# Where the 640 token columns of the split products are parted: 128 + 512 rather than 320 + 320

## The chip, the cores and the metric

The kernel runs on one core of one Trainium2 chip. The metric is the device time of one execution in microseconds. Inside the core five engines run their own instruction streams: TensorE (its matmuls are "PE" in the profile, its weight loads "PEld"), VectorE ("DVE"), ScalarE ("ACT"), GpSimd ("POOL") and SyncE ("SP"), the last of which issues most of the DMAs.

## What is computed

One step of a two-layer backbone over two groups of tokens that share all weights: 128 context tokens and 512 latent tokens, 640 in all, with a model width of 1024.

```python
for l in range(DEPTH):
    h = rmsnorm(x, g_pre_mix[l]) * (1.0 + sc1) + sh1      # sc, sh: one set per token group
    u = h @ w_in[l]                                       # q, k, v of attention; r, k, v of RWKV
    ...                                                   # windowed attention and RWKV scans
    x = x + gt1 * rmsnorm(concat(o_att, o_rw) @ w_o[l], g_post_mix[l])
    h = rmsnorm(x, g_pre_ffn[l]) * (1.0 + sc2) + sh2
    f = (silu(h @ w1) * (h @ w3)) @ w2                    # l = 0: dense, width 2816
    ...                                                   # l = 1: 8 experts of width 1408, top 2 of 8
    x = x + gt2 * rmsnorm(f, g_post_ffn[l])
```

All inputs, weights and outputs are float32. The context and the latent tokens differ in modulation, attention and scan, but the projections and the feed-forward are the same product for all 640.

## The kernel before

**The work and its order.** The phases follow each other: modulation, projection, attention, RWKV mixing, output projection and feed-forward of layer 0, then the same of layer 1 with the experts at the end. The weights stream from DRAM in blocks of 128 x 1024 float32 (512 KB) through a ring of 8 slots in SBUF. SyncE issues one block's DMA as soon as TensorE has counted the block 8 places earlier as used (`block_used`). The order of everything is written out by hand, each engine's stream on its own, tied by semaphores.

**Split products.** Large products do not run as full float32. ScalarE copies a block to the reduced float32 type (`fp32r` in the profile), the upper part (L1702, `w_proj`, `w_ffn`); VectorE subtracts it from the original and writes the lower part over the ring slot (L2278 in the projections and the experts, L2782 in the dense feed-forward, `ring_lo`). Activations are split alike (`hT_hi` or `hT_ffn_hi`, and `hT_lo`, L2284). `mm_split` (L449) then issues three matmuls into the same accumulator: upper times upper (L451), upper weights times lower activations (L452), lower weights times upper activations (L453). Each matmul comes with its own weight load.

**The 640-column helper.** `mm640_split` (L455) calls `mm_split` twice, for columns 0 to 320 and 320 to 640 of the token axis, with the weights as the stationary operand (128 x 128) and the activations as the moving one. Its accumulator is `pair_r(n)` (L445): 640 columns within the two PSUM banks 2n and 2n+1 (512 float32 columns each), columns 192 to 832 of the 1024, so that each half lies in one bank. Who uses the two:

- `proj_phase` of TensorE (L868): 21 blocks in each layer. For block o the 8 slices kc of 128 input channels are multiplied into pair `o % 4`. ScalarE's `proj_phase` (L1739) evicts a block when it has been used (L1750 and the lines after it for whole 640-column rows, L1763 and L1764 for the context and the latent part), and prepares the upper part of the block two further on; VectorE (L2371) reads the same pair once more for the token shift.
- `dense_phase` of TensorE (L1430): layer 0's feed-forward. In groups of 6, 6, 4 and 6 hidden tiles (`FF_GROUPS`) it computes two blocks per tile (w1 and w3), 44 in all, and after each group the down projection (`ff_down`, `ff_last`), which has 128 tokens as the stationary operand and 512 weight columns as the moving one. The pairs are given by `ff_pair`. ScalarE takes tanh of the w1 accumulator (L2096), VectorE combines it with the w3 one.
- `norm_into` (L848): the first block of each projection and of the dense feed-forward is interleaved with the transposes of the normalised input (L845): as soon as a slice kc of the input is transposed, evicted and split, its six products are issued.

The experts of layer 1 go through `mm_split` directly, with 256 moving columns (up) and 512 (down). Products of full float32 that cover all 640 tokens use another helper, `mm640` (L461), which issues 128 columns (L463) and 512 columns (L464).

Of the kernel before, what the change touches and what calls it, by code (L numbers as in the profile page):

```python
# [18 lines left out]
CTX = 128  # L19
LAT = 512  # L20
T = CTX + LAT
# [158 lines left out]
def build(nc, blocks, x_all, small, cond, sinkrows, router, low2, cache_k, cache_v, state, consts,  # L180
          y_all, new_k, new_v, new_state, h_rows, y_rows, h_plain):
    ctx = ExitStack()
    with ctx:
# [251 lines left out]
        def pair(n):  # L435

            return ps[:, 2 * n:2 * n + 2, :].rearrange("p b c -> p (b c)")
# [6 lines left out]

        def pair_r(n):  # L445

            return pair(n)[:, 192:832]

        def mm_split(nc, dst, w_hi, w_lo, m_hi, m_lo, start, stop):  # L449

            nc.tensor.matmul(dst, w_hi, m_hi, start=start, stop=False)  # L451
            nc.tensor.matmul(dst, w_hi, m_lo, start=False, stop=False)  # L452
            return nc.tensor.matmul(dst, w_lo, m_hi, start=False, stop=stop)  # L453

        def mm640_split(nc, n, w_hi, w_lo, h_hi, h_lo, start, stop):  # L455
            for h in range(2):
                sl = slice(320 * h, 320 * h + 320)
                mm = mm_split(nc, pair_r(n)[:, sl], w_hi, w_lo, h_hi[:, sl], h_lo[:, sl], start, stop)
            return mm

# [312 lines left out]
        def _(pe):  # L773
# [74 lines left out]
            def norm_into(k, first, w_h, hi):  # L848

                for kc in range(KC + 2):  # L850
                    if kc < KC:
                        norm_turn(k, kc)
                    j = kc - 2
                    if j >= 0:
                        if j == 0:
                            w_l = first_split()
                        pe.wait_ge(sem["x_lo"], first + j + 1)
                        at = slice(j * P, (j + 1) * P)
                        mm = mm640_split(nc, 0, w_h[:, at], w_l[:, at], hi[:, j, :], hT_lo[:, j, :], j == 0, j == KC - 1)
                done(mm)  # L860
# [7 lines left out]
            def proj_phase(l):  # L868
                norm_into(2 * l, X_PROJ[l], w_proj[:, used[0] % 2, :], hT_hi)
                for o in range(1, PROJ_B):  # L870
                    w_h, w_l = split_blk(w_proj)
                    n = l * PROJ_B + o
                    if o >= 4:
                        pe.wait_ge(sem["proj_ev_act"], n - 3)
                    if 6 <= o - 4 < 18:
                        pe.wait_ge(sem["proj_ev_dve"], 13 * l + o - 9)
                    for kc in range(KC):
                        k = slice(kc * P, (kc + 1) * P)
                        mm = mm640_split(nc, o % 4, w_h[:, k], w_l[:, k], hT_hi[:, kc, :], hT_lo[:, kc, :], kc == 0, kc == KC - 1)
                    done(mm)  # L880
# [549 lines left out]
            def dense_phase(l):  # L1430
                norm_into(2 * l + 1, X_FFN[l], ffn_high(used[0]), hT_ffn_hi)
                for g, (f0, f1) in enumerate(FF_GROUPS):
                    for f in range(f0, f1):
                        for w in range(2):
                            if f == 0 and w == 0:
                                continue
                            w_h, w_l = ffn_high(used[0]), first_split()
                            if f >= f0 + 2:
                                pe.wait_ge(sem["eh_g"], f - 1)
                            elif g >= 1:  # L1440
                                pe.wait_ge(sem["ff_dn"], 2 * NT * (g - 1) + 4 + 2 * (2 * (f - f0) + w))
                            for kc in range(KC):
                                k = slice(kc * P, (kc + 1) * P)
                                mm = mm640_split(nc, ff_pair(g, f, w), w_h[:, k], w_l[:, k], hT_ffn_hi[:, kc, :], hT_lo[:, kc, :], kc == 0, kc == KC - 1)
                            done(mm)
                    if g < len(FF_GROUPS) - 1:
                        ff_down(g, f0, f1)
                    else:
                        ff_last(g, f0, f1)
# [231 lines left out]
        def _(act):  # L1681
# [57 lines left out]
            def proj_phase(l):  # L1739
# [4 lines left out]
                for o in range(PROJ_B):  # L1744
                    act.wait_ge(sem["block_used"], first + o + 1)
                    if o + 2 < PROJ_B:
                        w_hi(w_proj, first + o + 2)
                    src = pair_r(o % 4)
                    if o < 4:
                        A(qT[:, o, :], src, ACT.Copy, scale=HD ** -0.5).then_inc(*E.sig("proj_ev_act"))  # L1750
                    elif o == 4:
                        A(kT[:, :], src, ACT.Copy).then_inc(*E.sig("proj_ev_act"))
                    elif o == 5:
                        A(vT[:, :], src, ACT.Copy).then_inc(*E.sig("proj_ev_act"))
                    elif o < 18:
                        j = o - 6
                        pr = praw[:, j % 2, :]
                        if j < 2:
                            for z in (0, 129, 642):
                                A(pr[:, z:z + 1], C("ones")[:, 0:1], ACT.Copy, scale=0.0).then_inc(*E.sig("act_step"))  # L1760
                        else:
                            act.wait_ge(sem["proj_ev_dve"], 13 * l + j - 1)
                        A(pr[:, 1:129], src[:, 0:CTX], ACT.Copy, scale=hpar[:, j:j + 1]).then_inc(*E.sig("act_step"))  # L1763
                        A(pr[:, 130:642], src[:, CTX:T], ACT.Copy, scale=hpar[:, j:j + 1]).then_inc(*E.sig("proj_ev_act"))  # L1764
                    elif o == 18:
                        A(zlow[:, 0, :], src, ACT.Tanh).then_inc(*E.sig("proj_ev_act"))
                    elif o == 19:
                        A(zlow[:, 1, :], src, ACT.Copy).then_inc(*E.sig("proj_ev_act"))
                    else:
                        A(zlow[:, 2, :], src, ACT.Tanh, scale=0.5).then_inc(*E.sig("proj_ev_act"))  # L1770
# [316 lines left out]
            def dense_phase(l):  # L2087
                first = FFN_AT[l]
                ff_w_hi(first + 2)
                for g, (f0, f1) in enumerate(FF_GROUPS):  # L2090
                    for f in range(f0, f1):
                        n = ff_blocks(g) + 2 * (f - f0)
                        act.wait_ge(sem["block_used"], n + 2)
                        if f >= 2:
                            act.wait_ge(sem["eh_g"], f - 1)
                        A(ftmp[:, f % 2, :], pair_r(ff_pair(g, f, 0)), ACT.Tanh, scale=0.5).then_inc(*E.sig("eh_th"))  # L2096
                        ff_w_hi(n + 3)
                        act.wait_ge(sem["eh_g"], f + 1)
                        A(g_hi[:, f - f0, :], g_f[:, f - f0, :], ACT.Copy).then_inc(*E.sig("eh_hi"))
                        ff_w_hi(n + 4)  # L2100
                    if g < len(FF_GROUPS) - 1:
                        for d in range(f1 - f0):
                            ff_w_hi(ff_blocks(g) + 2 * (f1 - f0) + d + 3)
# [1161 lines left out]
```

## Time and profile before

| | us |
|---|---|
| median of 2 runs | 2722.01 |
| lowest and highest | 2722.01 and 2722.01 |
| the profiled execution | 2724.16 |
| its span, first to last instruction | 2722.3 |
| mean granted clock of TensorE, share of full | 0.975 |

A record of a matmul or of a weight load begins when the hardware starts it and ends when it is through the array; the ends of matmuls are modelled, and successive records overlap. The distance between two starts is therefore a different quantity from the duration of one record. "f32" in a matmul's row stands for full and reduced float32 alike; which of the two it is follows from the line: L451 to L453 are the reduced type. A full float32 product appears as two records. In the waits, "A <- B" reads: A waited, and B ended it.

### The profile page before, as it was taken

Reading aid. Unit: us, or ns where it says so; the run is one execution under the profiler, and the core shown is the slowest. Engines: PE = TensorE matmul, PEld = TensorE weight load, DVE = VectorE, ACT = ScalarE, POOL = GpSimd, SP = SyncE. Lnnn points to the kernel's source line nnn. Section 1 sums busy time; section 2 is a strip of 40 time slices with the busy share of each in tenths; the row PEclk is TensorE's granted clock in tenths of the full one; section 3 lists DMA queues with packets and bytes.
Section 4 is the critical chain, followed back from the end, with each engine's and each line's share of the span. In section 5 each row is a group of like instructions: output and inputs, shape, how many; then the busy total and the mean of one; then the engine's idle time right before and its main releaser. Section 6 shows DMA issues by size and latency. Waiting matters only on the chain.

```text
span 2722.3 us, 68039 instructions
## 1 busy us (share of the span) xinstructions
PE 2521.7 (93%) x30324; PEld 2197.1 (81%) x30324; DVE 1401.3 (51%) x2474; ACT 1128.5 (41%) x2126; POOL 146.1 (5%) x163
## 2 busy tenths in 40 slices
PE   6998799898899999989987999998999999999996
PEld 3996577676798999969965777766899999999995
DVE  2337455556533333362374665474565555555565
ACT  3226544544421211242255545444444444444452
POOL 0002000010000000010010010001000000000011
PEclk8999899999999999999998999998999999999998
DMA  7223023320122222222200222202765666566672
GB/s 273 78 78 127 24 74 96 96 75 27 70 77 72 78 78 78 72 72 78 78 11 1 66 66 66 65 5 109 240 209 178 214 212 207 183 211 211 181 259 83
DMA packets 82701, 304.58 MB, mean 112 GB/s; under 512 B 9376, under 2 KB 9504, under 8 KB 82272
## 3 DMA queue, kind: packets, MB, share of 16 engines
q1 hardware_dynamic: 71072, 257.93, 29.6%
q0 software_dynamic: 11328, 42.21, 4.2%
q8 instruction: 241, 3.95, 0.6%
q14 instruction: 60, 0.49, 0.1%
HBM read 273.11 MB, written 27.00 MB: 110 GB/s over the span
## 4 chain that ended last, share of the span: by engine, by line
PE 83%; DVE 8%; issue 3%; ACT 3%; DMA 1%; POOL 0%; SPq 0%; another core or an unknown queue 0%; DVEq 0%; ACTq 0%; POOLq 0%
PE ps L451 19%; PE ps L452 19%; PE ps L453 19%; PE ps L1183 7%; PE ps L812 3%; PE ps L917 2%; PE ps L464 2%; PE ps L1115 2%; PE ps L960 1%; PE ps L976 1%; DMA ring<-in_blocks 1%; PE ps L463 1%; DVE arena L2474 1%; DVE arena L2473 1%; PE ps L1167 1%
## 5 line engine op out<-in xcount | busy, mean ns | idle before, releaser
L2278 DVE TENSOR_TENSOR ring_lo<-ring,w_ffn 128x1024 fp32r<-128x1024 f32 x264 | 322.5, 1225 | 214.5 <-ACT w_ffn L1702 208.5
L451 PE MATMUL ps<-hg_hi,w_ffn 128*128 128x256 f32 x1408 | 402.5, 286 | 3.2 <-DVE hg_lo L2909 3.2
L452 PE MATMUL ps<-hg_lo,w_ffn 128*128 128x256 f32 x1408 | 398.0, 283 | 0.0
L453 PE MATMUL ps<-hg_hi,ring_lo 128*128 128x256 f32 x1408 | 397.5, 282 | 0.0
L1702 ACT ACTIVATE w_ffn<-ring 128x1024 fp32r<-128x1024 f32 x264 | 278.1, 1057 | 197.7 <-PE ps L453 196.2
L451 PEld LDWEIGHTS ps<-hg_hi,w_ffn 128*128 128x128 f32 x1408 | 267.4, 190 | 4.8 <-DVE hg_lo L2909 3.4
L452 PEld LDWEIGHTS ps<-hg_lo,w_ffn 128*128 128x128 f32 x1408 | 266.5, 189 | 1.2
L453 PEld LDWEIGHTS ps<-hg_hi,ring_lo 128*128 128x128 f32 x1408 | 267.0, 190 | 0.0
L1183 PEld LDWEIGHTS ps<-arena 64*64 64x64 f32 x7680 | 165.0, 135 | 98.1 <-issue 78.5
L453 PE MATMUL ps<-hT_ffn_hi,ring_lo 128*128 128x320 f32 x704 | 216.0, 307 | 0.0
L1183 PE MATMUL ps<-arena 64*64 64x64 f32 x7680 | 190.5, 222 | 22.6 <-issue 22.2
L451 PE MATMUL ps<-hT_hi,w_proj 128*128 128x320 f32 x672 | 204.9, 305 | 6.7 <-DVE hT_lo L2284 6.6
L452 PE MATMUL ps<-hT_lo,w_proj 128*128 128x320 f32 x672 | 207.7, 309 | 0.0
L452 PE MATMUL ps<-hT_lo,w_ffn 128*128 128x320 f32 x672 | 207.6, 309 | 0.0
L453 PE MATMUL ps<-hT_hi,ring_lo 128*128 128x320 f32 x672 | 205.7, 306 | 0.0
L451 PE MATMUL ps<-hT_ffn_hi,w_ffn 128*128 128x320 f32 x672 | 203.4, 303 | 0.0
L451 PE MATMUL ps<-w_ffn,ge_hi 128*128 128x512 f32 x352 | 139.6, 397 | 9.3 <-DVE ring_lo L2278 9.3
L453 PE MATMUL ps<-w_ffn,ge_lo 128*128 128x512 f32 x352 | 138.8, 394 | 0.0
L2278 DVE TENSOR_TENSOR ring_lo<-ring,w_proj 128x1024 fp32r<-128x1024 f32 x42 | 51.3, 1225 | 169.2 <-ACT w_proj L1702 169.2
L452 PE MATMUL ps<-ring_lo,ge_hi 128*128 128x512 f32 x352 | 138.3, 393 | 0.0
L451 PEld LDWEIGHTS ps<-hT_hi,w_proj 128*128 128x128 f32 x672 | 126.1, 188 | 9.9 <-DVE hT_lo L2284 6.1
L453 PEld LDWEIGHTS ps<-hT_ffn_hi,ring_lo 128*128 128x128 f32 x704 | 132.6, 188 | 0.0
(375 smaller groups left out, 5107.1 us busy)
## 6 DMA issues: line engine op xcount, KB each, us to landing
ring<-in_blocks SPq DMA_DIRECT2D x484, 512.0 KB, 3.7
h_rows<-arena POOLq DMA_DIRECT2D x16, 512.0 KB, 10.2
arena<-h_rows POOLq DMA_DIRECT2D x7, 1024.0 KB, 9.9
y_rows<-arena POOLq DMA_DIRECT2D x7, 1024.0 KB, 6.6
x<-in_x_all SPq DMA_DIRECT2D x1, 2560.0 KB, 13.2
h_plain<-arena POOLq DMA_DIRECT2D x1, 2560.0 KB, 11.6
out_y_all<-x POOLq DMA_DIRECT2D x5, 512.0 KB, 3.7
w<-in_low POOLq DMA_DIRECT2D x2, 768.0 KB, 6.4
```

Source lines behind the costliest of these rows:

```text
L451: nc.tensor.matmul(dst, w_hi, m_hi, start=start, stop=False)
L452: nc.tensor.matmul(dst, w_hi, m_lo, start=False, stop=False)
L453: return nc.tensor.matmul(dst, w_lo, m_hi, start=False, stop=stop)
L463: nc.tensor.matmul(pair(n)[0:rows, 384:512], lhsT, rhs[:, 0:CTX], start=start, stop=stop)
L464: return nc.tensor.matmul(pair(n)[0:rows, 512:1024], lhsT, rhs[:, CTX:T], start=start, stop=stop)
L812: mm = nc.tensor.matmul(ps[32 * t:32 * t + 32, bank, :], cond32[:, kc, :], b[:, j * 512:(j + 1) * 512], start=kc < 4, stop=kc >= 4)
L917: return nc.tensor.matmul(flat[:, at:at + rhs.shape[1]], qT[rows64(g), c, tok], rhs, start=True, stop=False, skip_group_check=True)
L960: mm = nc.tensor.transpose(ps[:, 6, (j - a) * P:(j - a + 1) * P], prob[:, t % 3, j * P:(j + 1) * P], ident)
L1115: mm = nc.tensor.matmul(dst, xt[r, i, h, :], amv[r, i, h, :, :].rearrange("p a t -> p (a t)"), start=True, stop=True)
L1183: mm = nc.tensor.matmul(ps[rows64(to), 2 * b + s, at:at + CH], lhs[rows64(q), i, s, :], rhs[rows64(q), i, s, :], start=True, stop=True)
L1702: A(high[:, n % slots, :], ring[:, n % RING, :], ACT.Copy).then_inc(*E.sig("w_hi"))
L2278: V.tensor_tensor(ring_lo[:, n % RING, :], ring[:, n % RING, :], high[:, n % high.shape[1], :], ALU.subtract).then_inc(*E.sig("w_lo"))
```

## The change

The loop over two halves of 320 columns becomes a loop over the two token groups: columns 0 to 128 (context, `CTX` is 128) and 128 to 640 (latent, `T` is 640). The accumulator moves within its two banks, from columns 192 to 832 to columns 384 to 1024, so that again each part lies in one bank. All users of `pair_r` follow it, the evictions of ScalarE and VectorE included.

```diff
         def pair_r(n):
 
-            return pair(n)[:, 192:832]
+            return pair(n)[:, 384:1024]
 
         def mm_split(nc, dst, w_hi, w_lo, m_hi, m_lo, start, stop):
 
@@ -453,8 +453,7 @@
             return nc.tensor.matmul(dst, w_lo, m_hi, start=False, stop=stop)
 
         def mm640_split(nc, n, w_hi, w_lo, h_hi, h_lo, start, stop):
-            for h in range(2):
-                sl = slice(320 * h, 320 * h + 320)
+            for sl in (slice(0, CTX), slice(CTX, T)):
                 mm = mm_split(nc, pair_r(n)[:, sl], w_hi, w_lo, h_hi[:, sl], h_lo[:, sl], start, stop)
             return mm
```

## Rows read from the trace of the kernel before

**Rows 1.** The page: busy time, and the chain that ended last.

```profile
PE 2521.7 (93%) x30324; PEld 2197.1 (81%) x30324; DVE 1401.3 (51%) x2474; ACT 1128.5 (41%) x2126; POOL 146.1 (5%) x163
...
PE 83%; DVE 8%; issue 3%; ACT 3%; DMA 1%; POOL 0%; SPq 0%; another core or an unknown queue 0%; DVEq 0%; ACTq 0%; POOLq 0%
PE ps L451 19%; PE ps L452 19%; PE ps L453 19%; PE ps L1183 7%; PE ps L812 3%; PE ps L917 2%; PE ps L464 2%; PE ps L1115 2%; PE ps L960 1%; PE ps L976 1%; DMA ring<-in_blocks 1%; PE ps L463 1%; DVE arena L2474 1%; DVE arena L2473 1%; PE ps L1167 1%
```

**Rows 2.** Windows: PE, PEld, DVE, ACT, POOL busy (records), granted clock, DMA share, GB/s.

```profile
69.00:201.00 132.00, 132.00 (x915) 131.86 (x913) 42.30 (x54) 33.93 (x55) 0.00 (x0) 1.00 0.25 76
...
1230.00:1365.00 135.00, 134.48 (x932) 134.22 (x930) 42.32 (x54) 34.41 (x56) 0.00 (x0) 1.00 0.25 75
...
300.00:660.00 360.00, 319.39 (x8854) 246.81 (x8854) 197.85 (x445) 167.91 (x391) 28.80 (x22) 0.96 0.23 74
```

**Rows 3.** Waits (us, times, longest), 69 to 201 us; then 49 to 69.

```profile
ACT w_proj L1702 <- PE ps L453: 91.6, 18, 5.6
...
PE ps L451 <- DVE hT_lo L2284: 3.8, 5, 2.0
```

**Rows 4.** Groups of instructions, 69 to 201 us: busy, mean ns of one.

```profile
L453 PE MATMUL ps<-hT_hi,ring_lo 128*128 128x320 f32 x305 | 93.3, 306 | 0.0
```

**Rows 5.** Timeline in the first projection: start us, length us, what.

```profile
99.99 0.30 PE L451 MATMUL ps<-hT_hi,w_proj 128*128 128x320 f32 x1
100.00 0.19 PEld L452 LDWEIGHTS ps<-hT_lo,w_proj 128*128 128x128 f32 x1
100.13 0.31 PE L452 MATMUL ps<-hT_lo,w_proj 128*128 128x320 f32 x1
...
100.86 0.30 PE L451 MATMUL ps<-hT_hi,w_proj 128*128 128x320 f32 x1
```

**Rows 6.** Timeline of reduced products with 512 columns, in two stretches.

```profile
681.00 0.40 PE L451 MATMUL ps<-w_wo,oT_hi 128*128 128x512 f32 x1
...
682.38 0.40 PE L451 MATMUL ps<-w_wo,oT_hi 128*128 128x512 f32 x1
...
1051.19 0.40 PE L452 MATMUL ps<-ring_lo,g_hi 128*128 128x512 f32 x1
...
1051.89 0.40 PE L452 MATMUL ps<-ring_lo,g_hi 128*128 128x512 f32 x1
```

**Rows 7.** Timeline of reduced products with 256 columns (experts).

```profile
1944.45 0.28 PE L453 MATMUL ps<-hg_hi,ring_lo 128*128 128x256 f32 x1
...
1945.40 0.28 PE L452 MATMUL ps<-hg_lo,w_ffn 128*128 128x256 f32 x1
```

**Rows 8.** Timeline of two products of full float32.

```profile
1817.17 0.38 PE L463 MATMUL ps<-arena,w 128*128 128x128 f32 x2
1817.39 1.02 PE L464 MATMUL ps<-arena,w 128*128 128x512 f32 x2
```

**Rows 9.** Timeline of records with few columns; then the group of L820.

```profile
30.06 1.05 PE L820 MATMUL ps<-con,modrow 128*128 128x2 f32 x8
...
676.74 3.73 PE L1420 MATMUL ps<-arena,con 128*128 128x128 f32 x32
...
L820 PE MATMUL ps<-con,modrow 128*128 128x2 f32 x192 | 27.7, 265 | 4.5 <-ACT modrow L1709 3.4 <-issue 1.0
```

**Rows 10.** Groups of weight loads, whole span; then the timeline at bfloat16 products.

```profile
L451 PEld LDWEIGHTS ps<-hT_hi,w_proj 128*128 128x128 f32 x672 | 126.1, 188 | 9.9 <-DVE hT_lo L2284 6.1 <-issue 3.8
...
L1420 PEld LDWEIGHTS ps<-arena,con 128*128 128x128 f32 x64 | 7.5, 192 | 0.2
L931 PEld LDWEIGHTS ps<-con 128*128 128x128 bf16 x96 | 6.8, 97 | 15.3 <-issue 11.7
...
210.41 0.28 PE L931 MATMUL ps<-con 128*128 128x128 bf16 x2
...
210.54 1.08 PE L885 MATMUL ps<-arena,con 128*128 128x512 f32 x2
```

**Rows 11.** Group of ScalarE's latent evictions, 69 to 201 us: busy, mean ns.

```profile
L1764 ACT ACTIVATE arena<-ps,hpar 128x512 f32<-128x512 f32 x12 | 8.2, 680 | 0.0
```

## The prediction

> **What bounds the kernel now.** I read the page first. TensorE is busy 93% of the span, and its share of the chain that ended last is 83%, 57% of it on the three lines of the split product, L451 to L453 [rows 1]. The change touches those lines in two places only, so the next question is what limits these places. The stretches in which 320-column products run answer it: in the five long ones (69 to 201, 745 to 821, 862 to 946, 987 to 1043, 1071 to 1155 us) the matmul record is busy for the whole stretch, and in the sixth, 1230 to 1365 us, for all but 0.5 us; the granted clock is 1.00, while VectorE and ScalarE are busy a third of the time or less and the DMA share is 0.25 [rows 2] (the first and the last stretch stand there; the four between have the same pattern). What ScalarE and VectorE wait for there is TensorE itself: the next block's upper half waits for the last product of a block, 91.6 us in all in the first stretch, where TensorE has no row as the one that waits [rows 3]. So in these stretches the time is the number of matmuls times the distance from one start to the next.
>
> The duration of a record is no such distance. A 320-column product is listed with about 306 ns [rows 4], yet in the timeline starts follow each other after 140 to 150 ns [rows 5]: the records overlap. By count, 915 matmuls in 132 us are 144.3 ns apiece [rows 2]. Two triples of 320 columns, which is one kc step of a 640-token tile, take 6 x 144.3 = 866 ns; the timeline, with 99.99 to 100.86 for six starts, says 870 [rows 5].
>
> **How often.** A projection has 21 weight blocks in each of two layers, and layer 0's feed-forward 44, each of 8 kc steps: (42 + 44) x 8 = 688 steps. 3 blocks (24 steps) are the first of their phase and run interleaved with the normalisation's transposes, where TensorE waits now and then; 664 steps are in the dense stretches. The experts of layer 1 use 256 and 512 columns through the same lines but not through the 640-column helper, and do not change.
>
> **What the change does to one step.** Six products stay six, with the same six weight loads of 128 x 128; only the moving columns go from 320 x 6 to 128 x 3 and 512 x 3. The sum of columns is the same, 1920. The order becomes three short ones and then three long ones.
>
> The long ones have direct rows, the same reduced float32 type with 512 columns: six starts in 681.00 to 682.38 are 230 ns each, and the down projection at 1051.19 to 1051.89 has 233 [rows 6]. I take 231; 226 and 235 are the bounds (a shade beyond the two readings).
>
> The short ones have no row: no reduced product under 256 columns runs in this kernel. The nearest rows bound it. From below: going by columns alone, (231 - 144.3)/192 = 0.45 ns per column between 320 and 512, which puts 128 columns at 144.3 - 192 x 0.45 = 58 ns. From above, two rows. The narrowest reduced product, 256 columns, starts every 119 ns, 1944.45 to 1945.40 for eight [rows 7], and 128 columns should not take longer than 256 if nothing but width changes. A full float32 product is listed as two records where the code issues one matmul (L463 has 128 columns, L464 has 512), and its 128 columns take 220 ns, from 1817.17 to 1817.39 [rows 8]. Which end is near? Each product carries its own weight load, and the question is how fast these can follow each other. The answer is in the products that have almost no columns: L820 moves 2 columns with a 128 x 128 load, and eight such records span 1.05 us with a mean length of 0.265: (1.05 - 0.265)/7 = 112 ns apart. 32 records of 128 columns at L1420, if the last is as long, are (3.73 - 0.265)/31 = 112 ns apart [rows 9]. Records with 2 columns and with 128 are spaced alike, so what spaces those with 2 is the load. The loads of the reduced products look like the same thing: mean 188 ns, against 192 for L1420, while the bfloat16 load has 97 [rows 10]. In the timeline now a load starts with the product before it and is done under 320 columns [rows 5]; under 58 ns of columns it cannot be. After each short product the next one therefore waits for a load: 111 ns, bounds 108 and 120. After each long product the load is hidden and the columns set the pace.
>
> One step: 3 x 111 + 3 x 231 = 1026 ns against 866, that is 160 ns more. 664 x 0.160 = 106 us. Of the 24 interleaved steps part is absorbed by waits that are there already (TensorE waits 3.8 us in the first of the three blocks for the split of the normalised input [rows 3]); half of 24 x 0.16 gives 2 us. Together 108 us. The profiled execution took 2724.2 us for a span of 2722.3, so 2832 by its own measure; the median of the runs shown is 2722.0, 2.2 below it, and I give 2830.
>
> **The second edit**, the accumulator's place in its two banks (columns 384 to 1024 rather than 192 to 832), I cost at nothing. The evictions read as many columns; a 512-column part takes 0.68 us [rows 11] and the whole tile no more than twice that, once per block of 8 x 0.87 = 6.9 us, hidden under the products of the next block. Each half still lies in one bank. If the cover were gone it would be some 1.4 us per block, but the cover gets longer, as the block takes 8.2 us. The weight stream asks for less per us than now, and the block preparation likewise; nothing becomes late.
>
> **The rivals.** *No load limit.* If a short product follows its predecessor by its columns, a step is 3 x 58 + 3 x 231 = 867 ns, and nothing changes: 2722 us. If it costs what bfloat16 products of 128 columns do, of which two start in 210.41 to 210.54, 65 ns apiece [rows 10], a step is 888 ns and the time 2722 + 664 x 0.022 = 2737. This is the case on the other side (not slower by what can be told): its place is the load between two short products, and it decides as soon as that load needs under about 85 ns, where the total stays within 54 us. The equal column sum speaks for it; the 188 ns load and the L820 spacing speak against. [...]
>
> I give this rival 10%.
>
> *The reduced type falls back to full float32 cost for narrow products.* The records of full float32 are twice as many as the products, and 128 columns cost 220 ns. If the single-pass form holds only for wide moving operands (the rows have it at 256, 320 and 512 and nowhere below), a step is 3 x 220 + 3 x 231 = 1353, 487 more; 664 x 0.487 + 24 x 0.4 = 333 us, 3055. No row excludes it. Against it: at 256 columns there is no sign of a second pass, and the type is a property of the operand, not of its width. In the Trainium skill, "FP8 and Floating Point Precision" (TensorE Precision Notes) tells of true FP32 as four passes and of a reduced form that truncates what it reads; it names no width at which one becomes the other. 18%.
>
> *The clock falls.* The granted clock could leave its 2.4 GHz level in these stretches; at 1.2 GHz a step of 1026 ns doubles, 1.19 us more than now, about 3510 us. Against it, the stretch 300 to 660 us, where most products are of 64 x 64, keeps 0.96 [rows 2]. 2%. The remaining 4% is for costs between, such as a short product that also pays for the switch of bank or for a late long load (2860 to 2900).
>
> **How the numbers follow.** The load-limited case has 66%. Its own range: 3 x (108 + 226) = 1002 gives 136 ns and 90 us, 3 x (120 + 235) = 1065 gives 199 ns and 137 us with all 24 steps paid; 2813 to 2859. To reach 8 in 10 the range must take in the fall-back, so it runs from 2805 to 3065 and leaves out the unchanged case above all. About 2% is what a measurement can tell from no change: 54 us. Slower by more than that is 66 + 18 + 2 + 4 = 90%, less 1 for a load-limited case far under its lower bound; within 2% is that 1 and 9 of the first rival's 10; faster is the last 1%, as no step of the change removes work.
>
> **What would show it right or wrong.** In the changed kernel's timeline the short products should start 108 to 120 ns apart (58 to 66: first rival; 220: second), the long ones 226 to 235, and a block should take about 8.2 us. The stretches of rows 2 should stay at full busy with clock 1.00 and grow in proportion, the first projection by 25 us, each six-tile feed-forward group by 15; all other stretches should keep their lengths. If a stretch outside grows, or TensorE waits for ScalarE or VectorE inside, the account is wrong.

## The result and the profile after

The changed kernel takes 2829.8 us, median of two runs (2828.9 to 2830.7), against 2722.0: ratio 1.0396, 95% interval 1.0351 to 1.0441. The forecast was 2830. The lines below L455 are numbered one lower than before. The page of the changed kernel answers to [rows 1]: the same number of instructions, and TensorE as busy by its share.

```profile
span 2827.0 us, 68039 instructions
...
PE 2631.8 (93%) x30324; PEld 2215.7 (78%) x30324; DVE 1398.2 (49%) x2474; ACT 1128.9 (40%) x2126; POOL 146.7 (5%) x163
```

The busy time of the matmul record grew by 110 us, that of the weight loads by 19 only, and those of VectorE and ScalarE by nothing (VectorE's is 3 us less). Windows of the changed kernel, with the columns of [rows 2], inside the first projection, the first feed-forward group and the second projection:

```profile
93.00:230.00 137.00, 136.97 (x795) 118.72 (x793) 38.63 (x51) 28.99 (x49) 0.00 (x0) 1.00 0.20 62
777.00:858.00 81.00, 81.00 (x471) 70.40 (x471) 23.23 (x25) 16.55 (x20) 0.00 (x0) 1.00 0.22 65
1320.00:1471.00 151.00, 151.00 (x890) 133.01 (x889) 41.08 (x53) 32.27 (x53) 0.00 (x0) 1.00 0.20 63
```

TensorE is still busy throughout at clock 1.00, but only 795 products fit into 137 us: 172.3 ns each rather than 144.3. The DMA share fell from 0.25 to 0.20 because the blocks are asked for less often. The timeline of the changed kernel shows one step, which answers to [rows 5]:

```profile
100.64 0.23 PE L451 MATMUL ps<-hT_hi,w_proj 128*128 128x128 f32 x1
100.64 0.19 PEld L452 LDWEIGHTS ps<-hT_lo,w_proj 128*128 128x128 f32 x1
100.70 0.27 PE L452 MATMUL ps<-hT_lo,w_proj 128*128 128x128 f32 x1
100.75 0.19 PEld L453 LDWEIGHTS ps<-hT_hi,ring_lo 128*128 128x128 f32 x1
100.81 0.28 PE L453 MATMUL ps<-hT_hi,ring_lo 128*128 128x128 f32 x1
100.86 0.19 PEld L451 LDWEIGHTS ps<-hT_hi,w_proj 128*128 128x128 f32 x1
100.92 0.45 PE L451 MATMUL ps<-hT_hi,w_proj 128*128 128x512 f32 x1
100.97 0.19 PEld L452 LDWEIGHTS ps<-hT_lo,w_proj 128*128 128x128 f32 x1
101.21 0.39 PE L452 MATMUL ps<-hT_lo,w_proj 128*128 128x512 f32 x1
101.21 0.19 PEld L453 LDWEIGHTS ps<-hT_hi,ring_lo 128*128 128x128 f32 x1
101.44 0.40 PE L453 MATMUL ps<-hT_hi,ring_lo 128*128 128x512 f32 x1
...
101.67 0.23 PE L451 MATMUL ps<-hT_hi,w_proj 128*128 128x128 f32 x1
```

Read the loads first. Four of them start 0.11 us apart, from 100.64 to 100.97: each starts as soon as the one before it lets it, while the next two start with the long products they run under (the next is at 101.21). The step is 101.67 - 100.64 = 1.03 us. The matmul starts are shifted against this in a way that can mislead: the first short product is followed after only 60 ns and the first long one after 290 (100.92 to 101.21). A record begins some 60 ns after its own load has begun, when that load is still under way, so the first short product shows its column time and the first long record carries the rest of its load: 60 + 111 + 112 ns for the short three and 54 more in front of the long one, 337 ns or 3 x 112. The three long ones take 232 on average. (The starts of the loads part the same 1033 ns a little differently, 108, 111 and 112 ns after the short products; so the price of a load is known to some 4 ns.)

By stages, from the start of the first to the start of the last product of each, in the two profiled executions (spans 2722.3 and 2827.0):

| stage | before | after | difference | forecast |
|---|---|---|---|---|
| first projection | 151.5 | 180.2 | +28.7 | +26 |
| attention and RWKV mixing, layer 0 | 529.1 | 523.6 | -5.5 | 0 |
| feed-forward, four up groups | 312.1 | 369.7 | +57.6 | +56 |
| second projection | 151.6 | 176.8 | +25.2 | +26 |
| everything else | 1578.0 | 1576.7 | -1.3 | 0 |

### The profile page after: what moved, and what is told of

Read it like the earlier page. It is cut to its first block, busy times and chain, and to the rows that moved or that the text cites. A ratio compares the mean times of both kernels' runs of the same rounds, so it can differ in the third digit from the quotient of the medians.

```text
span 2827.0 us, 68039 instructions
## 1 busy us (share of the span) xinstructions
PE 2631.8 (93%) x30324; PEld 2215.7 (78%) x30324; DVE 1398.2 (49%) x2474; ACT 1128.9 (40%) x2126; POOL 146.7 (5%) x163
## 4 chain that ended last, share of the span: by engine, by line
PE 84%; DVE 8%; ACT 3%; issue 3%; DMA 1%; POOL 0%; another core or an unknown queue 0%; SPq 0%; DVEq 0%; ACTq 0%; POOLq 0%
PE ps L451 20%; PE ps L453 19%; PE ps L452 19%; PE ps L1182 6%; PE ps L811 3%; PE ps L463 2%; PE ps L916 2%; PE ps L1114 1%; PE ps L959 1%; PE ps L975 1%; DMA ring<-in_blocks 1%; PE ps L1083 1%; PE ps L462 1%; PE ps L1166 1%; DVE arena L2473 1%
## 5 line engine op out<-in xcount | busy, mean ns | idle before, releaser
L451 PE MATMUL ps<-hg_hi,w_ffn 128*128 128x256 f32 x1408 | 402.7, 286 | 3.7 <-DVE hg_lo L2908 3.7
L452 PE MATMUL ps<-hg_lo,w_ffn 128*128 128x256 f32 x1408 | 398.3, 283 | 0.0
L453 PE MATMUL ps<-hg_hi,ring_lo 128*128 128x256 f32 x1408 | 397.7, 282 | 0.0
L451 PEld LDWEIGHTS ps<-hg_hi,w_ffn 128*128 128x128 f32 x1408 | 267.8, 190 | 5.3 <-DVE hg_lo L2908 3.9
L452 PEld LDWEIGHTS ps<-hg_lo,w_ffn 128*128 128x128 f32 x1408 | 266.8, 189 | 1.2
L453 PEld LDWEIGHTS ps<-hg_hi,ring_lo 128*128 128x128 f32 x1408 | 267.3, 190 | 0.0
L453 PE MATMUL ps<-hT_ffn_hi,ring_lo 128*128 128x128 f32 x704 | 236.6, 336 | 0.0
L451 PE MATMUL ps<-hT_hi,w_proj 128*128 128x128 f32 (+1 forms) x672 | 226.0, 336 | 6.1 <-DVE hT_lo L2283 5.9
L451 PE MATMUL ps<-hT_ffn_hi,w_ffn 128*128 128x128 f32 (+1 forms) x672 | 225.6, 336 | 0.0
L453 PE MATMUL ps<-hT_hi,ring_lo 128*128 128x128 f32 (+1 forms) x672 | 224.7, 334 | 0.0
L452 PE MATMUL ps<-hT_lo,w_proj 128*128 128x128 f32 (+1 forms) x672 | 224.6, 334 | 0.0
L452 PE MATMUL ps<-hT_lo,w_ffn 128*128 128x128 f32 (+1 forms) x672 | 224.6, 334 | 0.0
L451 PE MATMUL ps<-w_ffn,ge_hi 128*128 128x512 f32 x352 | 139.6, 396 | 9.3 <-DVE ring_lo L2277 9.3
L2740 DVE SCALAR_TENSOR_TENSOR arena<-arena,ps 128x640 f32<-128x640 f32 x22 | 18.1, 821 | 261.6 <-ACT arena L2095 261.6
L451 PEld LDWEIGHTS ps<-hT_hi,w_proj 128*128 128x128 f32 x672 | 127.9, 190 | 23.2 <-DVE hT_lo L2283 5.4
L453 PEld LDWEIGHTS ps<-hT_ffn_hi,ring_lo 128*128 128x128 f32 x704 | 133.9, 190 | 15.5
L452 PEld LDWEIGHTS ps<-hT_lo,w_ffn 128*128 128x128 f32 x672 | 127.7, 190 | 15.5
```

## The experiments

The theory: a reduced product takes its columns' time, but the next one cannot start before its own 128 x 128 weight load is through, 112 ns after the load before it; only the load of the very next product runs beside a product. The rivals after the result: narrow reduced products are slow in themselves (two array cycles per column would, at 2.4 GHz, also give 107 ns at 128), and the place in the banks or the order matters. "Step" is the time of the products of one kc slice in the dense stretches of the profile, 866.7 ns before and 1033.3 after (1020.0 in the second projection).

**Other widths.** In these three, the boundary moves (a is 192, 224 or 256), the accumulator with it:

```diff
-            return pair(n)[:, 384:1024]
+            return pair(n)[:, 512 - a:1152 - a]
...
-            for sl in (slice(0, CTX), slice(CTX, T)):
+            for sl in (slice(0, a), slice(a, T)):
```

192 + 448:

> 192 + 448 columns. Load theory (a short product is followed no sooner than the next weight load allows, 112 ns; columns set the pace above that): 192 columns would need 87 ns by columns and still take 112, 448 take 202; a step of 6 products is 942 ns, 76 more than with 320 + 320, 664 steps give 50 us: 2772 us. Width rival (reduced products under 256 columns cost two array cycles per column, which also gives 107 ns at 128): 192 columns take about 172, a step is 1120 ns: about 2890 us.

Measured: 2775.2 us against 2726.4 on the same chip, ratio 1.0174 (1.0142 to 1.0206), 49 us more. The timeline of this kernel:

```profile
100.07 0.25 PE L451 MATMUL ps<-hT_hi,w_proj 128*128 128x192 f32 x1
100.16 0.28 PE L452 MATMUL ps<-hT_lo,w_proj 128*128 128x192 f32 x1
100.27 0.28 PE L453 MATMUL ps<-hT_hi,ring_lo 128*128 128x192 f32 x1
100.38 0.39 PE L451 MATMUL ps<-hT_hi,w_proj 128*128 128x448 f32 x1
...
101.01 0.25 PE L451 MATMUL ps<-hT_hi,w_proj 128*128 128x192 f32 x1
```

A step of 0.94 us (943 by the dense stretches, 942 expected), and the second and third short product are followed after 0.11 us, as with 128 columns, although they have half as many again. The width rival asked for 1120.

224 + 416:

> 224 + 416 columns. Load theory: 101 ns by columns, so still 112 by the load, and 187 for 416; a step of 897 ns, 2743 us. Width rival: 199 ns for 224 columns, a step of 1158 ns, about 2915 us, slower than 128 + 512.

Measured: 2745.7 us, ratio 1.0062 (1.0040 to 1.0084), 19 us more; the step is 903 ns against 897 expected. With more columns in the narrow part the time fell, where the width rival had it rise above that of 128 + 512. That rival is out.

256 + 384:

> 256 + 384 columns. Both theories: 119 and 173 ns, a step of 876 ns, 10 more than with 320 + 320: 2729 us. If the load still counted at 256 columns with more than the 119 ns seen in the experts, it would be slower than that.

Measured: 2731.5 us, ratio 1.0017 (0.9999 to 1.0035), which does not tell it from no change by time; the step does, 880 ns against 866.7 (876 expected), 664 x 13.3 = 9 us. At 256 columns the load is as good as covered.

**Short and long products in turn.**

```diff
-            for sl in (slice(0, CTX), slice(CTX, T)):
-                mm = mm_split(nc, pair_r(n)[:, sl], w_hi, w_lo, h_hi[:, sl], h_lo[:, sl], start, stop)
+            parts = (slice(0, CTX), slice(CTX, T))
+            for w, h, first, last in ((w_hi, h_hi, start, False), (w_hi, h_lo, False, False), (w_lo, h_hi, False, stop)):
+                for sl in parts:
+                    mm = nc.tensor.matmul(pair_r(n)[:, sl], w, h[:, sl], start=first, stop=last)
```

> 128 + 512 columns, but short and long products alternate instead of three short and three long ones, with the same stationary operand in the two of a pair. If only the load of the very next product can run beside a product, each short one still exposes one load: a step of 1032 ns as in the changed kernel, 2830 us. Rival (loads are fetched further ahead, or weights that are in place already are not waited for): the loads of two products fit into 232 + 60 ns, a step is about 866 to 880 ns, 2722 to 2735 us.

Measured: 2834.0 us against 2726.4, ratio 1.0389 (1.0355 to 1.0424), step 1027 ns. Its timeline, where equal lines are merged (x2 is a short and a long product):

```profile
100.24 0.50 PE L459 MATMUL ps<-hT_hi,ring_lo 128*128 128x128 f32 x2
100.35 0.42 PEld L459 LDWEIGHTS ps<-hT_hi,w_proj 128*128 128x128 f32 x2
100.58 0.50 PE L459 MATMUL ps<-hT_hi,w_proj 128*128 128x128 f32 x2
100.69 0.42 PEld L459 LDWEIGHTS ps<-hT_lo,w_proj 128*128 128x128 f32 x2
100.92 0.51 PE L459 MATMUL ps<-hT_lo,w_proj 128*128 128x128 f32 x2
```

Each pair takes 0.34 us, 112 + 232, three times a step. The two loads of a pair (224 ns) would fit under its products (290 ns by columns alone), and the stationary operand is the same in both, yet the load under the short product is waited for. So what counts is not the sum of loads against the sum of columns, but each load against the one product before it, and an operand that is in place already is loaded and waited for all the same. This run also answers a further rival. In the changed kernel the three short products add to the same accumulator columns one right after the other, and could be waiting for them. Here a long product into the other bank stands between them, and the step is nearly as long (1027 ns).

**Half the load.**

```diff
             for sl in (slice(0, CTX), slice(CTX, T)):
-                mm = mm_split(nc, pair_r(n)[:, sl], w_hi, w_lo, h_hi[:, sl], h_lo[:, sl], start, stop)
+                m = 64 if sl.start == 0 and not start and not stop else P
+                mm = mm_split(nc, pair_r(n)[0:m, sl], w_hi[:, 0:m], w_lo[:, 0:m], h_hi[:, sl], h_lo[:, sl], start, stop)
```

> As the changed kernel, but in the six middle kc steps of each block the short products load and use only 64 of the 128 weight columns (the other 64 output channels of the context tokens miss these terms). Same number of products and of moving columns. Load theory: the loads of the second and third short product halve and hide under 58 to 60 ns of columns, the load of the first long one stays whole: 60 + 60 + 112 + 3 x 232 = 928 ns in these steps, 1032 in the other two, 954 on average, 88 over 320 + 320: about 2781 us. Width rival (narrow reduced products are slow by themselves): nothing changes, 1032 ns and 2830 us.

Measured: 2782.2 us against 2718.2, ratio 1.0255 (1.0168 to 1.0343), average step 958 ns (954 expected). A step with halved loads in its timeline:

```profile
104.61 0.22 PE L451 MATMUL ps<-hT_hi,w_proj 128*64 128x128 f32 x1
104.61 0.13 PEld L452 LDWEIGHTS ps<-hT_lo,w_proj 128*64 128x64 f32 x1
104.66 0.22 PE L452 MATMUL ps<-hT_lo,w_proj 128*64 128x128 f32 x1
104.67 0.13 PEld L453 LDWEIGHTS ps<-hT_hi,ring_lo 128*64 128x64 f32 x1
104.72 0.22 PE L453 MATMUL ps<-hT_hi,ring_lo 128*64 128x128 f32 x1
104.72 0.19 PEld L451 LDWEIGHTS ps<-hT_hi,w_proj 128*128 128x128 f32 x1
104.78 0.45 PE L451 MATMUL ps<-hT_hi,w_proj 128*128 128x512 f32 x1
104.83 0.19 PEld L452 LDWEIGHTS ps<-hT_lo,w_proj 128*128 128x128 f32 x1
105.07 0.40 PE L452 MATMUL ps<-hT_lo,w_proj 128*128 128x512 f32 x1
```

The same 128 moving columns of the same type now follow after 55 to 60 ns, which is the lower bound of the prediction (58 ns, by columns alone). The edit changes two things at once: the load has 64 weight columns, and the product writes 64 partitions of the accumulator rather than 128. The third short product tells them apart. It is halved like the others, but the load behind it is a whole one, and it is paid for in full: 105.07 - 104.78 is 0.29 us rather than 0.23, and the loads themselves start 0.06 us apart at 104.61, 104.67 and 104.72, then 0.11 us to 104.83. So the distance goes with the next load and not with the short product's own form. This is the run that names the cause.

**No short products.**

```diff
             for sl in (slice(0, CTX), slice(CTX, T)):
+                if sl.start == 0 and not start and not stop:
+                    continue
```

> As the changed kernel, but the three short products of the six middle kc steps of each block are left out (the context tokens miss these terms). This prices them directly. Load theory: they cost three loads of 112 ns and nothing else, so these steps are 3 x 232 = 696 ns, 337 less than 1033; with two full steps of eight the average is 780, 86 under 320 + 320: 664 x 0.086 = 57 us, 2665 us. If part of the 167 ns came from the long products (a bank, a place, a late start), these steps would stay above 700.

Measured: 2638.5 us against 2711.2, ratio 0.972 (0.965 to 0.979). In its timeline the long products follow each other:

```profile
101.64 0.39 PE L451 MATMUL ps<-hT_hi,w_proj 128*128 128x512 f32 x1
...
102.34 0.39 PE L451 MATMUL ps<-hT_hi,w_proj 128*128 128x512 f32 x1
...
103.03 0.39 PE L451 MATMUL ps<-hT_hi,w_proj 128*128 128x512 f32 x1
```

Such a step takes 0.70 us (103.03 - 101.64 is 1.39 us for two), 693.5 ns on average over the profile against 696 expected. The short three therefore cost 1033.3 - 693.5 = 340 ns, within 4 of three loads. The two full steps of a block take 1020 ns each here, and the average of the eight is (6 x 693.5 + 2 x 1020)/8 = 775 ns (780 expected). The dense stretches give 664 x (866.7 - 775) = 61 us; the total fell by 73 against the kernel before on the same chip, where 57 had been expected. The other 12 us lie outside the changed stretches. In this profile attention and RWKV mixing of layer 0 were the shortest of all (518.4 us), and "everything else" of the table took 1559.7 us, where the other eleven profiles have 1562.1 to 1578.0. That is the scatter shown below or a little more, and what else may be in it, such as experts filled differently by the changed context tokens, was not looked into.

**The place and the order.**

```diff
-            return pair(n)[:, 384:1024]
+            return pair(n)[:, 0:640]
...
-            for sl in (slice(0, CTX), slice(CTX, T)):
+            for sl in (slice(0, 512), slice(512, T)):
```

> 512 + 128 columns, long products first, accumulator in columns 0 to 640 of its two banks. If the place in the banks and the order of the two parts have no part in it: a step of 1032 ns, 2830 us within 4. If the second edit of the change (the place) or the token-group boundary cost something, this run differs by it.

Measured: 2822.9 us against 2718.2, ratio 1.0405 (1.0300 to 1.0511), 105 us more; step 1033 ns. The median is 7 us under the 2830 that were expected within 4, and its two executions, 2816.3 and 2829.4 us, lie further apart than that; the step is the surer measure. By it, neither the place within the banks, nor which part comes first, nor the fact that the boundary is that of the token groups has a share.

**The feed-forward alone.** A second helper with the new loop and the new place serves `dense_phase`, its `norm_into` and the two evictions there; the projections keep the old one.

```diff
+        def mm640_group(nc, n, w_hi, w_lo, h_hi, h_lo, start, stop):
+            for sl in (slice(0, CTX), slice(CTX, T)):
+                mm = mm_split(nc, pair_g(n)[:, sl], w_hi, w_lo, h_hi[:, sl], h_lo[:, sl], start, stop)
+            return mm
...
-                                mm = mm640_split(nc, ff_pair(g, f, w), w_h[:, k], w_l[:, k], hT_ffn_hi[:, kc, :], hT_lo[:, kc, :], kc == 0, kc == KC - 1)
+                                mm = mm640_group(nc, ff_pair(g, f, w), w_h[:, k], w_l[:, k], hT_ffn_hi[:, kc, :], hT_lo[:, kc, :], kc == 0, kc == KC - 1)
```

> 128 + 512 in layer 0's feed-forward alone (44 blocks, 344 dense steps and 8 interleaved ones), 320 + 320 in the projections. 344 x 0.167 = 57 us and about 1: 2780 us, each six-tile group 15.9 us longer. Attention and RWKV mixing of layer 0 run before the first changed product, so their stretch should be the 529 us of the kernel before; the changed kernel had them 5.5 us shorter. If they come out shorter here too, that difference has nothing to do with the change.

Measured: 2771.7 us against 2718.2, ratio 1.0217 (1.0125 to 1.0308), 53 us more (57 and 1 expected; the step is 1033.3 ns in the feed-forward and 866.7 in both projections). The windows of this kernel, in the first projection, in layer 0's attention and RWKV mixing, and in the second feed-forward group:

```profile
69.00:201.00 132.00, 132.00 (x915) 131.85 (x913) 42.32 (x54) 33.92 (x55) 0.00 (x0) 1.00 0.25 76
...
200.80:722.80 522.00, 465.86 (x9899) 354.16 (x9898) 304.83 (x693) 261.61 (x621) 51.26 (x56) 0.97 0.23 77
...
870.90:969.80 98.90, 98.90 (x577) 86.00 (x576) 27.46 (x31) 17.79 (x21) 0.00 (x0) 1.00 0.21 65
```

The first projection is as before to the record, the second group is as in the changed kernel. The stretch between them came out at 522 us, not at the 529 expected, although nothing in front of it differs from the kernel before. So the 5.5 us that this stretch had given back in the changed kernel are no effect of the change. It varies by itself: over the twelve profiles of this study it lies between 518.4 and 540.1 us, with the same work in it. The longest is that of 256 + 384, where the granted clock was 0.94 against 0.97 above. The three longest (532.5, 534.2 and 540.1 us) have granted clocks of 0.95, 0.94 and 0.94; but at 0.97 the stretch still lies anywhere from 518 to 525 us, so the clock is not all of it.

```profile
204.50:744.70 540.20, 480.31 (x9899) 366.35 (x9897) 305.27 (x693) 261.49 (x621) 51.26 (x56) 0.94 0.22 74
```

The totals of the kernel before scatter too, with medians of 2722.0, 2726.4, 2718.2 and 2711.2 us in the four sets of runs, and there as well the longer executions have the lower mean clock: 2700.7 us at 0.978, 2737.1 at 0.969. In which stretches these executions differ isn't shown, as they were not profiled; so each run is compared with the kernel before of its own set.

**320 + 320 in other orders.** Is there something to gain from how the loads fall in the kernel before? First the alternating order there (the loop of the experiment above, with 320 + 320):

> 320 + 320 columns as in the kernel before, but the two halves alternate, so that each stationary operand is loaded twice in a row for two products. In the kernel before a product is followed after 140, 148 or 145 ns, 140 where the next load is of the same operand. If that is the reason, half of the six distances become 140 and the step falls from 867 to about 855, 2714 us; if all of them, 840, 2704 us. If the load is hidden and plays no part, 867 and no change.

Measured: 2719.5 us against 2711.2, ratio 1.0036 (1.0010 to 1.0061), slightly slower; the step is 880 ns, 13 more. None of the three expected steps (855, 840, or 867 unchanged) came: loading the same operand twice in a row doesn't shorten the distance, and the order does play a part.

Then another order of the three products:

```diff
-                mm = mm_split(nc, pair_r(n)[:, sl], w_hi, w_lo, h_hi[:, sl], h_lo[:, sl], start, stop)
+                nc.tensor.matmul(pair_r(n)[:, sl], w_hi, h_lo[:, sl], start=start, stop=False)
+                nc.tensor.matmul(pair_r(n)[:, sl], w_hi, h_hi[:, sl], start=False, stop=False)
+                mm = nc.tensor.matmul(pair_r(n)[:, sl], w_lo, h_hi[:, sl], start=False, stop=stop)
```

> 320 + 320 columns, with the product of the lower activations first and that of the upper ones second. The same six operand pairs in another order: if the 140, 148 and 145 ns belong to the operands, the step stays 867 ns within 3 and the time does not change; if they belong to the order (same operand next, another next), it can move by up to 26 ns, 17 us, either way.

Measured: 2709.1 us against 2711.2, ratio 0.9994 (0.9979 to 1.0010), step 866.7 ns as before. Its timeline has the same three distances, and they stand at the same places of the triple, not with the same operands:

```profile
99.87 0.30 PE L458 MATMUL ps<-hT_lo,w_proj 128*128 128x320 f32 x1
100.01 0.31 PE L459 MATMUL ps<-hT_hi,w_proj 128*128 128x320 f32 x1
100.16 0.31 PE L460 MATMUL ps<-hT_hi,ring_lo 128*128 128x320 f32 x1
100.30 0.30 PE L458 MATMUL ps<-hT_lo,w_proj 128*128 128x320 f32 x1
```

The product after which the same stationary operand comes again is followed after 140 ns, whichever it is (here `hT_lo`, before `hT_hi`), the next after 148. What makes the 140, and why alternating halves lose by it, stays open. No version here beats 320 + 320.

## Why the prediction was right

- *The bound.* The stretches with 640-column products were read as TensorE's alone, number of products times distance. They grew by 111.5 us in sum; VectorE and ScalarE have no more work there than before, and TensorE has no row as the one that waits in 90 to 229 us. In the changed kernel the block preparation waits still longer for TensorE, 102.3 us in 16 waits between 90 and 229 us, 6.4 us each, where before it was 91.6 us in 18 [rows 3], 5.1 each:

```profile
ACT w_proj L1701 <- PE ps L453: 102.3, 16, 6.9
DVE ring_lo L2277 <- ACT w_proj L1701: 92.0, 16, 7.4
```

- *The count.* 664 dense steps and 24 interleaved ones held.
- *The short products.* 111 ns were taken from products with 2 columns and from loads of the same length (188 and 192 ns). They measured 337/3 = 112 with 128 columns, 112 to 113 with 192 and 224, and 58 to 60 once the load was halved. The sign that the prediction named for them was worded too simply, though: it said that the short products would start 108 to 120 ns apart and the long ones 226 to 235. The first short one is followed after 60 ns, inside the range given to the first rival, and the first long one after 286. Only the sum over a step, or the starts of the loads, decides between the two. The inference that a load sets the pace, drawn from rows of another operation, was the step that could have gone wrong: the column sum alone gave no change, the full float32 price gave 3055.
- *The long products.* 231 ns expected, 232 found in five of the six stretches. In the second projection the step was 1020 and not 1033 ns, in which the long ones had 227 to 230; this was within the bounds of 226 to 235 and took 2 us off.
- *The step.* 160 ns more were predicted, 166.7 came in 504 steps and 153.3 in 160: 84.0 + 24.5 = 108.5 us against 106.
- *The interleaved steps.* 2 us were taken, 3 came (111.5 - 108.5). Some 2 of the 3 are in the first projection. There the clock of the changed kernel fell to its lower level for a few us, where before had 1.00 throughout; 51 to 55 us has a mean of 0.59:

```profile
51.00:55.00 4.00, 4.00 (x19) 3.52 (x18) 2.05 (x3) 1.72 (x3) 0.00 (x0) 0.59 0.00 0
```

  At that level the load is no longer 112 ns. Short products of this stretch are followed after 0.21 and 0.22 us, the long one at 52.20 after 0.43:

```profile
51.24 0.41 PE L452 MATMUL ps<-hT_lo,w_proj 128*128 128x128 f32 x1
51.45 0.41 PE L453 MATMUL ps<-hT_hi,ring_lo 128*128 128x128 f32 x1
51.67 0.73 PE L451 MATMUL ps<-hT_hi,w_proj 128*128 128x512 f32 x1
52.20 0.63 PE L452 MATMUL ps<-hT_lo,w_proj 128*128 128x512 f32 x1
52.63 0.63 PE L453 MATMUL ps<-hT_hi,ring_lo 128*128 128x512 f32 x1
```

- *What the forecast owes to luck.* The changed stretches cost 111.5 us, 3.5 more than forecast. The attention stretch gave back 5.5 us, which is no effect of the change, and everything else 1.3. The last 3 us lie between the profiled executions (2724.2 and 2828.9) and the medians. 2830 against 2829.8 is closer than the method is: the attention stretch alone lay between 518 and 540 us in the profiles above.
- *The second edit* was costed at nothing, and the long-first run, with yet another place and the same step, shows it so.
- *The rivals.* "No load limit" had the right lower bound, 58 ns, for products without the load; with it the case is out. "Falls back to full float32 cost" is out at every width tried, 128, 192 and 224: going by columns the reduced type takes 58, 86 and 101 ns there, 0.45 ns a column, as at 320 and 512 (144 and 232 ns), where one cycle at 2.4 GHz is 0.42. "The clock falls" is out as well: it stayed at 1.00 in the dense stretches.

The load rule as the Trainium skill has it ("TensorE: Matmul & The Clock Gate", section "LDWEIGHTS", columns divided by 1.2, in ns) gives an estimate of 107 ns for 128 columns and 53 for 64. At clock 1.00 the traces show 108 to 112, and no more than 60. The Trainium skill also says on that page (section "Weight-path perf modes") that the fast load is on for 128 weights of any type but FP32. For the reduced float32 type it does not show here: 188 to 190 ns per load record, about as for full float32 (192), where the bfloat16 load has 97 [rows 10].

## What to carry to other kernels

The price of a matmul in a dense stream is the larger of two times: its own columns, and the weight load of the product behind it, which runs beside this one product only. With reduced float32 weights of 128 columns the load is 112 ns at clock 1.00, and 112 ns is what some 250 columns take at 0.45 ns each, so parts narrower than that waste time on it (224 + 416 still cost 37 ns per step, 256 + 384 cost 13); divide a width that exceeds one bank evenly, and don't hope that a long neighbour covers a short part. And take the distance between starts from the timeline, not the length of a record: a row's mean of 306 ns stood for 144 ns of time.

## What was not expected of the hardware

The long products have more than one pace. With the same code and operands of the same shape the three (L451, L452, L453) were followed after 286, 232 and 233 ns in the first projection of the changed kernel, after 280, 230 and 227 in the second, and in the half-load run after 286, 235 and 236. In the changed kernel each held constant over the dense part of its stretch, all at clock 1.00. In the timeline of the second projection:

```profile
1400.01 0.22 PE L451 MATMUL ps<-hT_hi,w_proj 128*128 128x128 f32 x1
...
1400.29 0.44 PE L451 MATMUL ps<-hT_hi,w_proj 128*128 128x512 f32 x1
...
1400.57 0.39 PE L452 MATMUL ps<-hT_lo,w_proj 128*128 128x512 f32 x1
```

The first long product is followed after 0.28 us here. The kernel before shows the same range with 512 columns, 230 and 233 ns [rows 6], but not with 320, whose step was 866.7 ns in all six stretches. The cause was not sought.

Loading the same stationary operand for two products in a row is neither skipped nor cheaper, and with 320 + 320 in turn it cost 13 ns per step.
